# Single-tile chunks with homes outside the ring at two layer changes, one more mixed pair, and moved waits

## What is computed

```python
x = x + gate[:, None, :] * rms_norm(y, post_g[i])   # end of layers 1 and 2; y = ... @ w_out
h = rms_norm(x, pre_g[i]) * (1 + scale[:, None, :]) + shift[:, None, :]   # start of the next
...
h2 = rmsnorm(x, norm_ffn[l])
x = x + jnp.square(jax.nn.relu(h2 @ w_up[l])) @ w_down[l]
```

## Time and profile before

| | us |
|---|---|
| median of 3 runs | 2552.17 (2549.19 to 2552.95) |
| the profiled execution | 2551.69 |
| its span | 2549.9 |
| TensorE busy | 2498.6 |
| DVE busy | 1871.5 |
| ACT busy | 1405.4 |
| mean granted clock of TensorE | 0.997 of full |

### The profile page before, as it was taken

How to read it: one execution, slowest core, us unless ns; L and a number is a source line. 1 busy time by engine, 2 the same in 40 slices (tenths; PEclk the granted TensorE clock), 3 DMA queues, 4 the chain that set the end, 5 groups by cost and what they waited for, 6 DMA issues and landing times.

```text
span 2549.9 us, 32959 instructions
## 1 busy us (share of the span) xinstructions
PE 2498.6 (98%) x11904; PEld 2066.8 (81%) x11904; DVE 1871.5 (73%) x2786; ACT 1405.4 (55%) x1955; POOL 436.7 (17%) x288
## 2 busy tenths in 40 slices
PE   5999999999999999998999999999999999999999
PEld 4888888888887888887887777888888888888887
DVE  7899787866677777766655555557887878888864
ACT  4555764444447555555466666655555545545543
POOL 0165563111021000010000000024111111111111
PEclk9999999999999999999999999999999999999999
DMA  9989777978784867654545455454656464646464
GB/s 348 330 291 336 246 254 272 321 279 288 249 290 151 242 200 211 196 181 151 181 152 176 151 164 165 151 179 150 223 172 221 160 232 164 226 170 216 164 215 148
DMA packets 355643, 549.11 MB, mean 215 GB/s; under 512 B 32332, under 2 KB 126128, under 8 KB 355120
## 3 DMA queue, kind: packets, MB, share of 16 engines
q1 hardware_dynamic: 353680, 541.24, 63.3%
q10 hardware_dynamic: 1824, 6.04, 0.6%
HBM read 545.13 MB, written 2.10 MB: 215 GB/s over the span
## 4 chain that ended last, share of the span: by engine, by line
PE 90%; DVE 3%; issue 3%; ACT 2%; DMA 1%; POOL 0%; SPq 0%; DVEq 0%; ACTq 0%; POOLq 0%
PE ps L2186 48%; PE ps L2191 24%; PE ps L2213 2%; PE ps L2212 2%; PE ps L2216 2%; PE ps L2171 1%; PE ps L2173 1%; PE ps L2172 1%; DMA raw<-in_sgu_w_in 1%; ACT hi L533 1%; DVE ps L1216 1%; PE ps L2265 1%; PE ps L2555 1%; DVE lo L1187 1%; PE ps L2788 1%
## 5 line engine op out<-in xcount | busy, mean ns | idle before, releaser
L1187 DVE TENSOR_TENSOR lo<-raw,hi 128x1024 fp32r<-128x1024 f32 x550 | 715.9, 1317 | 396.8 <-ACT hi L533 396.4
L533 ACT ACTIVATE hi<-raw 128x1024 fp32r<-128x1024 f32 x550 | 575.8, 1058 | 459.6 <-PE ps L2191 359.3
L2186 PE MATMUL ps<-hi,a_hi 128*128 128x512 f32 (+1 forms) x2016 | 801.2, 397 | 1.9 <-issue 1.0
L2186 PE MATMUL ps<-hi,a_lo 128*128 128x512 f32 (+1 forms) x2016 | 787.0, 390 | 0.0
L2191 PE MATMUL ps<-lo,a_hi 128*128 128x512 f32 (+1 forms) x2016 | 539.4, 390 | 0.0
L520 ACT ACTIVATE hi<-raw 128x1024 fp32r<-128x1024 f32 x336 | 355.0, 1060 | 293.7 <-PE ps L2191 261.3
L1163 DVE TENSOR_TENSOR lo<-raw,hi 128x1024 fp32r<-128x1024 f32 x336 | 421.8, 1273 | 124.0 <-ACT hi L520 122.2
L2186 PEld LDWEIGHTS ps<-hi,a_hi 128*128 128x128 f32 x2016 | 379.2, 188 | 82.2 <-issue 3.8
L2191 PEld LDWEIGHTS ps<-lo,a_hi 128*128 128x128 f32 x2016 | 378.8, 188 | 79.3
L2186 PEld LDWEIGHTS ps<-hi,a_lo 128*128 128x128 f32 x2016 | 379.5, 188 | 73.6
L2186 PE MATMUL ps<-hi,b_hi 128*128 128x512 f32 x896 | 354.7, 396 | 1.1 <-DVE b_lo L1275 0.8
(11 more groups left out here) (339 smaller groups left out, 2577.0 us busy)
## 6 DMA issues: line engine op xcount, KB each, us to landing
raw<-in_ada_w SPq DMA_DIRECT2D x96, 1024.0 KB
raw<-in_sgu_w_in SPq DMA_DIRECT2D x96, 1024.0 KB
raw<-in_w_up SPq DMA_DIRECT2D x64, 1024.0 KB
raw<-in_w_down SPq DMA_DIRECT2D x64, 1024.0 KB
raw<-in_w_in SPq DMA_DIRECT2D x42, 1024.0 KB
raw<-in_sgu_w_out SPq DMA_DIRECT2D x32, 1024.0 KB
raw<-in_w_in SPq DMA_DIRECT2D x128, 256.0 KB
raw<-in_mla_w_in SPq DMA_DIRECT2D x33, 512.0 KB
```

The lines of the kernel that those rows point to most:

```text
L533: nc.scalar.activation(hi[:, q % CHUNKS, :], raw[:, r % RAWS, q % 2 * CW:(q % 2 + 1) * CW], ACT.Copy).then_inc(hi_ready, 1)
L1187: nc.vector.tensor_tensor(lo[:, q % CHUNKS, :], raw[:, r % RAWS, q % 2 * CW:(q % 2 + 1) * CW], hi[:, q % CHUNKS, :].bitcast(F32), ALU.subt ...
L2186: nc.tensor.matmul(ps[:, 2 * s + t, 0:width], x[:, k0 + j, t * P:(t + 1) * P], hi[:, c, w], start=begins, stop=False)
```

## The change

1. First change of layer: all eight chunks of the last block go by tiles. Chunks 4 to 7 (numbers 252 to 255) have homes in `b_hi`/`b_lo`, which are free there; ACT does not wait for `chunk_used` for them.
2. Second change: six chunks by tiles (2 to 7); the last two (368, 369) have homes in `spare_hi`/`spare_lo`, which lie over the second tile of v.
3. The first two of the last four blocks become a pair, the 17th, on banks 6, 7, 0, 1, 2 and 3. Its sums of x are made in the two pairs before it.
4. In the first pair the turns of groups 6 and 7 move from behind chunks 3 and 5 to behind 5 and 6, on all three engines. In the third pair the wait for `t_lo` behind chunk 0 is gone.

```diff
-    ("down", 2, p) for p in range(2)) + tuple(("last", 3, b) for b in range(4))
+    ("down", 2, p) for p in range(2)) + (("down", 3, 0),) + tuple(("last", 3, b) for b in range(2, 4))
...
-MIX_BANKS = ((2, 3, 0, 1), (0, 1, 2, 3))
+MIX_BANKS = ((2, 3, 0, 1, 6), (0, 1, 2, 3, 6)) * 8 + ((6, 7, 0, 1, 2),)
...
+SPARE_1, SPARE_2 = (252, 253, 254, 255), (368, 369)
...
-        v = sb("v", [P, T, W2])
+        with nc.sbuf_tensor("v", [P, T, W2], F32) as v:
+            pass
+        sb("v_first", [P, W2])
+        spare_hi, spare_lo = (ctx.enter_context(nc.sbuf_tensor(k, [P, 2, CW], F32R)) for k in ("spare_hi", "spare_lo"))
...
+        def home(q, high):
+
+            if q in SPARE_1:
+                k = 4 * (q - SPARE_1[0])
+                return (b_hi if high else b_lo)[:, k:k + 4, :].rearrange("p k s -> p (k s)")
+            if q in SPARE_2:
+                return (spare_hi if high else spare_lo)[:, q - SPARE_2[0], :]
+            return (hi if high else lo)[:, q % CHUNKS, :]
...
-            act.wait_ge(chunk_used, n.chunk.at(ahead + 1))
-            nc.scalar.activation(hi[:, q % CHUNKS, :], raw[:, r % RAWS, q % 2 * CW:(q % 2 + 1) * CW],
+            if q not in SPARE_1 + SPARE_2:
+                act.wait_ge(chunk_used, n.chunk.at(ahead + 1))
+            nc.scalar.activation(home(q, True), raw[:, r % RAWS, q % 2 * CW:(q % 2 + 1) * CW],
...
+            act_mixed_pair(act, n)
+            for b in range(2):
+                act_steps(act, n, 8, last=(b == 1))
...
-            dve_steps(dve, n, 32, last=True)
+                between = turning((b_hi, b_lo), p)
+                between[15] = (lambda: dve_sums_lo(dve, 6, 0)) if p else lambda: dve_sums(dve, n, (b_hi, b_lo))
+                dve_mixed_pair(dve, n, None, between)
+            dve_mixed_pair(dve, n)
+            dve_steps(dve, n, 16, last=True)
...
-            for c in range(4):
-                pe_chunk(pe, n, A, 1, 2 * c, 2, NB, False, False)
-            pe_by_tiles(pe, n, A, 1, range(8, 16, 2), ends=True, tells=True, before={(1, 0): columns})
+            assert n.chunk.base + 4 == SPARE_1[0]
+            pe_by_tiles(pe, n, A, 1, range(0, 16, 2), ends=True, tells=True, before={(1, 0): columns})
...
-            for c in range(4):
+            for c in range(2):
                 pe_chunk(pe, n, B, banks, turned_place(2 * c), 2, NB, c == 0, False)
-            pe_by_tiles(pe, n, B, banks, [turned_place(k) for k in range(8, 16, 2)], ends=True, tells=True)
+            assert n.chunk.base + 4 == SPARE_2[0]
+            pe_by_tiles(pe, n, B, banks, [turned_place(k) for k in range(4, 16, 2)], ends=True, tells=True)
...
-            pe_mixed_pair(pe, n, A, 1, 1, {3: lambda: mixed(6), 5: lambda: mixed(7), 8: lambda: pe.wait_ge(t_lo, n.tg.base),
+            pe_mixed_pair(pe, n, A, 1, 1, {5: lambda: mixed(6), 6: lambda: mixed(7), 8: lambda: pe.wait_ge(t_lo, n.tg.base),
...
-            pe_mixed_pair(pe, n, B, 0, 2, {0: lambda: pe.wait_ge(t_lo, n.tg.base), 3: lambda: added(6), 5: lambda: added(7),
+            pe_mixed_pair(pe, n, B, 0, 2, {3: lambda: added(6), 5: lambda: added(7),
...
-            for b in range(3):
-                pe_block(pe, n, B)
+            pe_mixed_pair(pe, n, B, 0, 6)
+            pe_block(pe, n, B)
```

More of the change, by code:

```diff
@@ L721, in act_mixed_pair @@
                     act.wait_ge(acc_free, n.acc.at(4))
-                    nc.scalar.activation(first_kept, ps[:, MIX_BANKS[place.pair % 2][0], :], ACT.Copy).then_inc(p1_kept, 1)
+                    nc.scalar.activation(first_kept, ps[:, MIX_BANKS[place.pair][0], :], ACT.Copy).then_inc(p1_kept, 1)
                 if up is not None and s in (13, 14):
@@ L1142, in _ @@
             for p in range(2):
[L1143 to L1146, removed]
+                between = {s: (lambda g=4 * p + i: hidden(b_hi, g)) for i, s in enumerate(TURN_AFTER)}
+                if p:
+                    between[3] = lambda: act_sums(act, 6, 0)
+                late = act_mixed_pair(act, n, None, between, late)
+            act_mixed_pair(act, n)
+            for b in range(2):
+                act_steps(act, n, 8, last=(b == 1))
+                if b < 1:
                     act_result(act, n, None)
@@ L2222, in pe_mixed_pair @@
             pair = FFN_PLACES[n.chunk.base].pair
-            b11, b21, b5, b6 = MIX_BANKS[pair % 2]
+            b11, b21, b5, b6, b12 = MIX_BANKS[pair]
             own = lambda k, t: lambda j: tuple(a[:, k + j, t * P:(t + 1) * P] for a in x2)
@@ L2325, in pe_tile_chunk @@
         def pe_tile_chunk(pe, n, x2, s, k0, kts, width, t, ahead, begins, ends):
-            c = (n.chunk.base + ahead) % CHUNKS
+            q = n.chunk.base + ahead
             out_ = ps[:, 2 * s + t, 0:width]
@@ L2332, in pe_tile_chunk @@
             for j, w in enumerate(parts):
[L2333 to L2334 removed]
+                nc.tensor.matmul(out_, x2[0][:, k0 + j, rows_], home(q, True)[:, w], start=begins and j == 0, stop=False)
+                nc.tensor.matmul(out_, x2[1][:, k0 + j, rows_], home(q, True)[:, w], start=False, stop=False)
             pe.wait_ge(lo_ready, n.chunk.at(ahead + 1))
             for j, w in enumerate(parts):
[L2337 removed]
+                ins = nc.tensor.matmul(out_, x2[0][:, k0 + j, rows_], home(q, False)[:, w], start=False, stop=ends and j == kts - 1)
             return ins
@@ L2345, in pe_by_tiles @@
                         before[t, c]()
-                    ins = pe_tile_chunk(pe, n, x2, s, k0, kts, width, t, c, begins and c == 0, ends and c == 3)
+                    ins = pe_tile_chunk(pe, n, x2, s, k0, kts, width, t, c, begins and c == 0, ends and c == len(places) - 1)
                     if t:
                         ins.then_inc(chunk_used, 1)
-                    if tells and c == 3 and t == 0:
+                    if tells and c == len(places) - 1 and t == 0:
                         ins.then_inc(half_done, 1)
-            n.chunk.base += 4
+            n.chunk.base += len(places)
         def pe_pair(pe, n, i, t, p, normal, free, freed):
```

30 lines of the change are left out of this document (13 added, 17 removed).

## The result

The changed kernel took 2555.85 us (median of 20 runs, 2553.25 to 2560.63), the kernel before 2551.47 us (20 runs, 2549.19 to 2556.08). The ratio is 1.0018, with a 95% interval of 1.0012 to 1.0024: 4.4 us slower, which is just under what I called a visible difference (0.2%). The forecast was 2556.5 us (range 2549.0 to 2559.5), which is +4.9 us against the profiled execution of the kernel before.

The account below looks back on a forecast made before the run. TensorE, busy 98% of the span, was taken to bound the kernel, through matmul count and waits. +5.44 + 0 + 1.5 + 0 - 1.36 - 0.7 = +4.9 on 2551.69 gave 2556.6, say 2556.5 us, range 2549.0 to 2559.5.

Parts of the forecast that it names:

- term 1: First change of layer: tile 0 done no earlier, waiting for DVE's lo halves, 24 more matmuls behind it, +5.44 us.
- The bound without POOL: First change's block: if POOL did not slow DVE's lo half of chunk 4, 4.4 us in place of 5.44.
- The other bound: First change's block: a pass that never waits, so the old wait goes too, -0.60 us.
- Term 2: Behind the first change's block: an earlier tile 0 gains nothing, 0, at best about 0.3 us of idle.
- Term 3: First change's block: holes bring a half-clock spell, only its part behind 779.65 costs, +1.5 us, between 0 and 3.4.
- Rival (b): First change: a long half-clock spell beginning near 779.65 costs 3.4 in place of 1.5, total 2558.5 us; chance 0.18.
- Term 4: Second change of layer: tile 0 done 2.72 us earlier, block's end stays, 0; bounds -1.7 and +0.2 us.
- Term 5: Added pair in the last four blocks: 186 matmuls in place of 192, all covered, -1.36 us; upper bound +1.4.
- rival (c): Added pair not covered, costing as much as it saves or more, total about 2558.5 us; chance 0.08.
- Term 6: Regrouped waits: 0 in the first pair, the third pair's 0.81 us wait goes, -0.7 us; bounds -0.8 and -0.3.

Follow-up runs that it names:

- the sums early and POOL out of the way: Changed kernel with the last two ada slabs summed ahead of chunks 248 and 250, and POOL's block 2 work on 8 columns: ratio 0.9993 to the kernel before.
- the first change alone: Kernel before with only all eight chunks by tiles at the first change of layer: ratio 1.0016 to the kernel before.
- the early root: Changed kernel with tile 0's root (ACT) and normalizing (DVE) put ahead of tile 1's work at both changes of layer: ratio 1.0005 to the kernel before.

## Why the prediction was right, and where it was not

- **Bound and term 1.** +5.44 forecast, +5.38 measured, with tile 0 done 17.15 us after the start, as before. The waits were 3.06 and, where no half-clock stretch filled the second hole, 2.64 us (about 3.0 and 2.8 forecast). The runs confirm the reason, DVE's order: with the sums early and POOL out of the way the same pass runs with no wait that the profile names, and the block is as short as before. The bound without POOL, 4.4, was too high: I took 1.07 us for POOL's share, from one lo half, and it is 2.3, since two instructions of the ada sum were slowed as well (the one at 774.44 by 0.79 us, the one at 772.74, 1.12 us, by 0.38). I had also read the 1.23 us of chunk 3's lo half as DVE without POOL: the size is right, but POOL was at work there too, and it was POOL that waited. The other bound, -0.60 for a pass that never waits, came out at -0.14, since two small delays stay.
- **Term 2** came out at 0 (1.82 us from the end to the turns in both). Its bound was too small: I gave the lead 0.3 us at best, the early root took 0.7 from it. I had counted the idle time in front of the turns and not that DVE, free of tile 0, is earlier with tile 1.
- **Term 3, the clock, is the one that failed as a number**: +1.5 forecast, 0 in the profiled execution of the change, 1.49 in that of the first change alone. That a stretch comes, and that only its part behind the holes costs, was right; one price for it was wrong. It depends on where the 3.4 us fall: between the holes they were free, at the end of the last hole they cost nearly their half. It is also not the only one: the stretch near 803, behind the same block, was there in 5 of 14 profiles and cost 0.9 to 1.3 us, and it is missing in kernels with and without the change. Rival (b), the long spell, was in no profile of the starved pass.
- **Term 4** came out at 0, with the lead of 2.72 us and the block's length as forecast, and its bound of -1.7 was what the lead is worth, once the order lets it be used.
- **Term 5**: -1.36 forecast, -1.36 and -1.35 measured. "No earlier pair waits", in rival (c), is true of the pairs without turns alone: the first and third have a wait each.
- **Term 6**: -0.7 forecast, about -0.2 measured. In the first pair the forecast of 0 was +0.3; the new wait is the one that I had named as tight. In the third the wait went, -1.08 with its start-up, but "tight by some 0.1 us" behind ACT's root was wrong: the root itself had to wait for DVE's variance, and 0.6 came back. I had looked at ACT's order there and not at what its root waits for.
- **The sum.** The misses of term 3 (-1.5, or 0) and term 6 (+0.5) partly cancel; that the sum of 4.9 is so near the 4.4 of the medians is in part luck. The medians, with an interval from 3.1 to 6.1 us, can't tell a term 3 of 0 from one of 1.5; the profiled execution, whose steps add up to 3.5, can.

## What to carry to other kernels

A tile that is done earlier is worth nothing until each engine's order lets its next steps run in that time: look at which instruction stands ahead of the next step on ACT and DVE, and change lead and order together, since here either alone gave nothing or cost. Cutting work into pieces that use up operands twice as fast can move the limit to whoever makes the operands; count that engine's work over the whole pass, with what other duties and neighbours on the same memory take from it. And compare single profiles by the step of the shift across a place, not by their ends: here 4.3 us of the 7.9 between the two spans came from ahead of the change.

## What the hardware did that I had not expected

- The half-clock stretches move from execution to execution even where the order of instructions is the same: the one near 803 us was absent, 3.4 us or 6.8 us long. Where it was 6.8 us it cost no more than 1.3 us. TensorE waits for part of that time anyway, which would explain it, but this was not tried. The one at the second change was there in all 14 profiles, mostly 6.8 us long. In the starved pass it came in all four, although there were bursts of matmuls between the holes. The Trainium skill (TensorE: Matmul & The Clock Gate, HAM oscillation) tells of a kernel that waited for data between bursts and was throttled again at every wait; here only one stretch came for two holes, and it cost 0 or 1.5 us.
- POOL's cost on DVE is not only in the one instruction that it meets: with the lo halves back to back, DVE ran at about half its rate for as long as POOL worked, over 8 us, and POOL's two products took 3.64 us in place of 2.95. Each of the two waits for the instruction of the other that began first.
